# Differential attention among fp32 projections: paired scores, a buffer for four blocks of probabilities, and steps of ScalarE and VectorE in another order

## What is computed

```python
q1 = partial_rope(rmsnorm(qh[..., :64], g_q));  q2 = ...(qh[..., 64:])
k1 = partial_rope(rmsnorm(kh[..., :64], g_k));  k2 = ...(kh[..., 64:])
# for each block of 128 queries, mask: chunk(key) <= chunk(query), chunks of 64
s1 = einsum('bhqd,bhkd->bhqk', q1, k1) / 8
s2 = einsum('bhqd,bhkd->bhqk', q2, k2) / 8
p = softmax(where(mask, s1, NEG_INF)) - lam * softmax(where(mask, s2, NEG_INF))
o_b = rmsnorm(einsum('bhqk,bhkd->bhqd', p, v), g_sub) * (1 - lambda_init)
```

## Time and profile before

| | |
|---|---|
| median of 3 runs | 2455.0 us (2454.37 to 2455.52) |
| profiled execution | 2456.67 us |
| its span, first to last instruction | 2454.8 us |
| TensorE busy | 2385.6 us, 97% |
| VectorE, ScalarE, GpSimd busy | 1309.3 (53%), 870.2 (35%), 239.3 (10%) us |
| mean granted TensorE clock | 0.991 |

### The profile page before, as it was taken

One profiled execution on the slowest core, in us unless ns is written; L12 is line 12 of the kernel. 1 busy time (PEld: TensorE's weight loads), 2 busy tenths in 40 slices (PEclk: granted clock), 3 DMA queues, 4 the chain that ended last, 5 costly groups with the idle time before them and its releaser, 6 DMA issues.

```text
span 2454.8 us, 33629 instructions
## 1 busy us (share of the span) xinstructions
PE 2385.6 (97%) x11140; PEld 1906.9 (78%) x11148; DVE 1309.3 (53%) x1859; ACT 870.2 (35%) x1349; POOL 239.3 (10%) x225
## 2 busy tenths in 40 slices
PE   6999999999999999999999999999999999999997
PEld 4777667888888787776878888887888787888886
DVE  4443665654343559885546455465544545544554
ACT  2454344543232442214333222234444333322222
POOL 3001110112000110001112000021000302000003
PEclk8999999999999999999999999999999999999999
DMA  3111112333333433330213333333121222333332
GB/s 117 52 47 48 52 52 70 98 116 94 94 95 94 121 101 95 111 111 27 85 43 94 96 101 94 94 87 86 53 59 52 65 64 60 103 93 95 99 92 83
DMA packets 394557, 202.36 MB, mean 82 GB/s; under 512 B 13626, under 2 KB 392683, under 8 KB 394474
## 3 DMA queue, kind: packets, MB, share of 16 engines
q1 hardware_dynamic: 393136, 198.56, 27.6%
q0 software_dynamic: 1008, 2.62, 0.3%
q10 hardware_dynamic: 330, 0.08, 0.0%
HBM read 199.11 MB, written 2.10 MB: 82 GB/s over the span
## 4 chain that ended last, share of the span: by engine, by line
PE 88%; DVE 4%; issue 3%; ACT 2%; DVEq 1%; POOLq 0%; DMA 0%; ACTq 0%; SPq 0%; POOL 0%
PE bank L1614 23%; PE bank L1616 22%; PE bank L1615 22%; PE bank L1598 2%; PE bank L1972 2%; PE bank L1964 2%; PE bank L1992 2%; DVE m_w_lo L996 1%; PE bank L2180 1%; PE bank L2071 1%; PE bank L2047 1%; PE bank L2152 1%; PE bank L1733 1%; PE bank L1709 1%; PE bank L1745 1%
## 5 line engine op out<-in xcount | busy, mean ns | idle before, releaser
L517 ACT ACTIVATE m_w_hi<-m_raw 128x1024 fp32r<-128x1024 f32 x341 | 361.3, 1060 | 963.2 <-PE bank L1616 924.2
L1614 PE MATMUL bank<-m_h_hi,m_w_hi 128*128 128x512 f32 x1504 | 619.1, 412 | 9.8 <-DVE m_h_lo L1035 5.8
L1616 PE MATMUL bank<-m_h_hi,m_w_lo 128*128 128x512 f32 x1504 | 588.4, 391 | 0.0
L1615 PE MATMUL bank<-m_h_lo,m_w_hi 128*128 128x512 f32 x1504 | 587.4, 391 | 0.0
L996 DVE TENSOR_TENSOR m_w_lo<-m_raw,m_w_hi 128x1024 fp32r<-128x1024 f32 x341 | 472.7, 1386 | 75.8 <-ACT m_w_hi L517 72.5
L1614 PEld LDWEIGHTS bank<-m_h_hi,m_w_hi 128*128 128x128 f32 x1504 | 283.8, 189 | 83.9 <-issue 25.2
L1616 PEld LDWEIGHTS bank<-m_h_hi,m_w_lo 128*128 128x128 f32 x1504 | 283.0, 188 | 61.1
L1615 PEld LDWEIGHTS bank<-m_h_lo,m_w_hi 128*128 128x128 f32 x1504 | 284.0, 189 | 57.6 <-issue 5.8
L1614 PE MATMUL bank<-m_f_hi,m_w_hi 128*128 128x512 f32 x688 | 269.8, 392 | 2.9 <-DVE m_w_lo L996 2.7
L1616 PE MATMUL bank<-m_f_hi,m_w_lo 128*128 128x512 f32 x688 | 267.8, 389 | 0.0
L1615 PE MATMUL bank<-m_f_lo,m_w_hi 128*128 128x512 f32 x688 | 267.8, 389 | 0.0
(11 more groups left out here) (342 smaller groups left out, 3142.0 us busy)
## 6 DMA issues: line engine op xcount, KB each, us to landing
m_raw<-in_ff_w SPq DMA_DIRECT2D x256, 256.0 KB, 3.0
m_raw<-in_w_in SPq DMA_DIRECT2D x48, 256.0 KB, 3.1
m_raw<-in_conv_pw_w SPq DMA_DIRECT2D x48, 256.0 KB, 4.0
m_raw<-in_w_ffn_gate SPq DMA_DIRECT2D x44, 256.0 KB, 3.1
m_raw<-in_w_ffn_up SPq DMA_DIRECT2D x44, 256.0 KB, 3.2
m_raw<-in_w_ffn_down SPq DMA_DIRECT2D x40, 256.0 KB, 3.0
m_raw<-in_w_gate SPq DMA_DIRECT2D x32, 256.0 KB, 2.9
m_mem_w<-in_mem_wk SPq DMA_DIRECT2D x32, 256.0 KB, 3.1
```

Of the source, the lines that this page charges most:

```text
L517: act.activation(WH[:, v % 2], RAW[:, v % 2], ACT.Copy).then_inc(s.w_hi, 1)
L1614: pe.matmul(o, WH[:, r, k, :], hi, start=start, stop=False)
L1615: pe.matmul(o, WH[:, r, k, :], lo, start=False, stop=False)
L1616: last = pe.matmul(o, WL[:, r, k, :], hi, start=False, stop=stop)
```

## The change

- **TensorE, scores:** `sc(b)` issues both score matmuls, then both masks.
- **TensorE, order:** both `bd` at hook 0.5. `sc(2)` goes from 9 to 8.5, `vt` from 7 to 9.5, `sc(3)` from 11 to 10.5, `tr(0)` from 9 to 11.5, `av(0)` and `tr(1)` to 12.5, `av(1)` from 12 to 13.5, `tr(2)` from 12.5 to 14. `av(2)`, `tr(3)` go from 14 to -0.5 of the next group, `av(3)` from 15 to 1 of it, `turned_o` from 4.5 to 7.
- **Buffer:** `PC` holds the combined probabilities of all four blocks, 1280 columns; `cm` writes there and `tr` reads there.
- **ScalarE:** `squares` and the root of the head before are taken out of `roots` and put behind it, in the first and second list; `pt(3)` goes into the next group; `ex`, `turned_v` and `pt` are in a later and other order.
- **VectorE:** `step` has a second list, `between`, issued between a unit's evacuation and the next split; `mx(3)`, `cm(2)` are in it for the third unit. `on` and `ol` go to the second unit's list, around `mx(0)`, `mx(1)`; `cm(1)` to the third's.

```diff
--- before.py
+++ after.py
@@ -225,6 +225,8 @@
         P1 = at("da_p1", 164, [P, 2, T])
         P2 = at("da_p2", 168, [P, 2, T])
         SQD = at("da_sq", 172, [P, 2, T])
+        BLOCKS = [P * t * (t + 1) // 2 for t in range(QB + 1)]
+        PC = at("da_pc", 72, [P, BLOCKS[QB]])
 
         def staging(tag, kb):
             return [at(f"{tag}_{n}", kb + 2 * i, [P, T]) for i, n in
@@ -635,20 +637,12 @@
 
             def da_pieces(n, prev):
                 def roots():
-
-                    if prev is not None:
-                        squares(prev)
-                        act.drain()
                     for t in range(2):
                         act.wait_ge(s.da_ms, n * 2 + (t + 1))
                         act.activation(RSD[t][:], SBK[t][:], ACT.Ln, bias=EPSC)
-                    if prev is not None:
-                        root_log()
                     act.drain()
                     for t in range(2):
                         act.activation(RSD[t][:], RSD[t][:], ACT.Exp, scale=-0.5).then_inc(s.da_rs, 1)
-                    if prev is not None:
-                        root_exp()
 
                 def ex(b):
                     def f():
@@ -660,17 +654,18 @@
                                            accum_out=ST[:, 8 * b + 2 + c:8 * b + 3 + c]).then_inc(s.da_exp, 1)
                     return f
 
...
-                return [[roots],
-                        da_late(prev)[1:] + [turned_v(V, s.da_vt, s.da_v, n), ex(0), ex(1)],
-                        [pt(0), ex(2), pt(1), ex(3)],
-                        [pt(2), pt(3)]]
+                late = da_late(prev)
+                return [late[0:1] + [roots] + late[1:2],
+                        late[2:3] + [ex(0)] + late[3:],
+                        [ex(1), turned_v(V, s.da_vt, s.da_v, n), ex(2), da_pt(n, 0)],
+                        [ex(3), da_pt(n, 1), da_pt(n, 2)]]
+
+            def da_pt(n, b):
+                def f():
+                    w = (b + 1) * P
+                    act.wait_ge(s.da_tr, n * 4 + (b + 1))
+                    act.activation(PT[:, b % 2, 0:w], TR[:, 0:w], ACT.Copy).then_inc(s.da_pt, 1)
+                return f
 
@@ -686,9 +681,11 @@
 
             def da_late(n):
 
-                def on():
+                def power():
                     squares(n)
                     act.drain()
+
+                def root():
                     root_log()
                     act.drain()
                     root_exp()
@@ -696,7 +693,7 @@
                 def oh():
                     act.wait_ge(s.da_g, n + 1)
                     act.activation(pick(OBH, n), DT2[:], ACT.Copy).then_inc(s.da_oh, 1)
-                return [] if n is None else [on, oh]
+                return [] if n is None else [da_pt(n, QB - 1), power, root, oh]
 
             def then(pieces, late):
                 return [late + pieces[0]] + pieces[1:] if late else pieces
@@ -714,7 +711,7 @@
             with U.loop(act, PAIRS - 2, 4) as i:
                 group([None] * 4, da_pieces(i + 1, i))
             group([None] * 4, da_pieces(PAIRS - 1, PAIRS - 2))
-            group([None] * 4, [da_late(PAIRS - 1), [], [], []])
+            group([None] * 4, [da_late(PAIRS - 1)[0:2], da_late(PAIRS - 1)[2:], [], []])
             act.wait_ge(s.gates_in, 1)
 
 
@@ -996,13 +993,15 @@
                 dve.tensor_tensor(WL[:, v % 2], RAW[:, v % 2], WH[:, v % 2].bitcast(F32), ALU.subtract)\
                     .then_inc(s.w_lo, 1)
 
-            def step(evac, before=()):
+            def step(evac, before=(), between=()):
                 for piece in before:
                     piece()
                 n = U.take()
                 if evac is not None:
                     dve.wait_ge(s.unit_done, U.count(n + 1))
                     evac(GB[n % 2], bank_free[n % 2])
+                for piece in between:
+                    piece()
                 if n + 2 < TOTAL:
                     split(n + 2)
 
@@ -1036,9 +1035,9 @@
                                              in1=pick(hi, m).bitcast(F32), op0=ALU.mult, op1=ALU.subtract)\
                         .then_inc(s.xg_lo, 1)
 
-            def group(evacs, pieces):
+            def group(evacs, pieces, between=((),) * 4):
                 for j, e in enumerate(evacs):
-                    step(e, pieces[j] if pieces else ())
+                    step(e, pieces[j] if pieces else (), between[j])
 
 
             for k in range(KD):
@@ -1176,25 +1175,25 @@
                 def cm(b):
                     def f():
                         w = (b + 1) * P
-                        a, c = P1[:, b % 2, 0:w], P2[:, b % 2, 0:w]
+                        a, c, out = P1[:, b % 2, 0:w], P2[:, b % 2, 0:w], PC[:, BLOCKS[b]:BLOCKS[b + 1]]
                         r = ST[:, 8 * b + 6:8 * b + 8]
                         dve.wait_ge(s.da_exp, n * 8 + (2 * b + 2))
                         dve.reciprocal(r, ST[:, 8 * b + 2:8 * b + 4])
                         dve.drain()
                         dve.tensor_scalar(c, c, r[:, 1:2], LAM, ALU.mult, ALU.mult)
                         dve.drain()
-                        dve.scalar_tensor_tensor(out=a, in0=a, scalar=r[:, 0:1], in1=c,
+                        dve.scalar_tensor_tensor(out=out, in0=a, scalar=r[:, 0:1], in1=c,
                                                  op0=ALU.mult, op1=ALU.subtract).then_inc(s.da_p, 1)
                     return f
 
                 late = da_late(prev)
-                return [[gained(0), gained(1)] + late[0:1] + [rope(0), rope(1)],
-                        late[1:] + [mx(0), mx(1), cm(0), cm(1)],
-                        [mx(2), cm(2), mx(3)],
-                        [cm(3)]]
+                return [[gained(0), gained(1), rope(0), rope(1)],
+                        late[0:1] + [mx(0), mx(1)] + late[1:] + [cm(0)],
+                        [cm(1), mx(2)],
+                        [cm(3)]], ((), (), [mx(3), cm(2)], ())
 
             def then(pieces, late):
-                return [late + pieces[0]] + pieces[1:]
+                return [late + pieces[0][0]] + pieces[0][1:], pieces[1]
 
             def gate(c):
                 return scaled(pick(GATES, c))
@@ -1238,11 +1237,11 @@
             with U.loop(dve, PAIRS - 2, 4) as i:
                 group(sb_evacs(i + 2, (s.sb_vt, i + 2)), sb_pieces(i + 1, i))
             group(da_evacs(0, (s.sb_vt, PAIRS)), sb_pieces(PAIRS - 1, PAIRS - 2, False))
-            group(da_evacs(1, (s.da_vt, 1)), then(da_pieces(0, None), sb_late(PAIRS - 1)))
+            group(da_evacs(1, (s.da_vt, 1)), *then(da_pieces(0, None), sb_late(PAIRS - 1)))
             with U.loop(dve, PAIRS - 2, 4) as i:
-                group(da_evacs(i + 2, (s.da_vt, i + 2)), da_pieces(i + 1, i))
-            group([gate(8 + j) for j in range(4)], da_pieces(PAIRS - 1, PAIRS - 2))
-            group([gate(12 + j) for j in range(4)], [da_late(PAIRS - 1), [], [], []])
+                group(da_evacs(i + 2, (s.da_vt, i + 2)), *da_pieces(i + 1, i))
+            group([gate(8 + j) for j in range(4)], *da_pieces(PAIRS - 1, PAIRS - 2))
+            group([gate(12 + j) for j in range(4)], [[], da_late(PAIRS - 1), [], []])
             dve.drain().then_inc(s.gates_in, 1)
 
             with U.loop(dve, 4, 2) as i:
@@ -1755,8 +1754,32 @@
                         13.5: [c(1, 2)], 14.5: [c(1, 3)]}
                 return merged_hooks(mine, sb_late(prev)) if prev is not None else mine
 
+            def da_tr(n, b):
+                def f():
+                    pe.wait_ge(s.da_p, n * 4 + (b + 1))
+                    if b == 0:
+                        pe.wait_ge(s.da_v, n + 1)
+                    else:
+                        pe.wait_ge(s.da_pt, n * 4 + b)
+                    for j in range(b + 1):
+                        last = turn(TR[:, j * P:(j + 1) * P], PC[:, BLOCKS[b] + j * P:BLOCKS[b] + (j + 1) * P])
+                    last.then_inc(s.da_tr, 1)
+                return f
+
+            def da_av(n, b):
+                def f():
+                    pe.wait_ge(s.da_pt, n * 4 + (b + 1))
+                    if b == 0 and (not isinstance(n, int) or n > 0):
+                        pe.wait_ge(s.da_on, n)
+                    for j in range(b + 1):
+                        last = pe.matmul(OB[:, b * P:(b + 1) * P], PT[:, b % 2, j * P:(j + 1) * P], V[:, j, :],
+                                         start=(j == 0), stop=(j == b))
+                    last.then_inc(s.da_av, 1)
+                return f
+
             def da_late(n):
-                return {4.5: [turned_o(ON, s.da_on, n + 1, s.da_ot)]}
+                return {-0.5: [da_av(n, 2), da_tr(n, 3)], 1: [da_av(n, 3)],
+                        7: [turned_o(ON, s.da_on, n + 1, s.da_ot)]}
 
             def da_hooks(n, prev):
                 def vt():
@@ -1788,39 +1811,17 @@
                         if b >= 2:
                             pe.wait_ge(s.da_exp, n * 8 + (2 * b - 2))
                         for c in range(2):
-                            bank = SBK[(2 * b + c) % 4]
```

(12 more changed lines are left out.)

## The result

| | before | after |
|---|---|---|
| median of 5 runs | 2455.0 us | 2440.3 us (2439.74 to 2442.62) |
| ratio, 95% interval | | 0.9943 (0.9931 to 0.9955) |
| profiled execution | 2456.67 us | 2439.74 us |
| its span | 2454.8 us | 2437.6 us |
| stretch S (below) | 185.3 us | 170.3 us |

The forecast was 2443.4 us, with 2438.5 to 2450.5 as the range, 11.6 us less than before; 14.7 us less were measured. One of the five executions of before took 2687.7 us and is not among the runs that the ratio compares.

The account below looks back on a forecast made before the run. TensorE, busy 97% of the span, was taken as the bound. Paired scores (8.6 us) plus fewer waits (3.0) save 11.6 us: profiled 2456.7 becomes 2445.1, median 1.7 lower, 2443.4; range 2438.5 to 2450.5.

Parts of the forecast that it names:

- The pairing, 8.6 us: In each sc, both scores before both masks save a load, mask switching and one pass: 2.15 us a group, 8.6 in all.
- three passes: In each sc, the two scores' four fp32 passes take the time of three; chance 0.50, 2441 to 2446 us.
- the one from neighbours in the queue to neighbours in time: In sc, passes issued A1, A2, B1, B2 (A, B the row halves): only neighbours A2 and B1 overlap, saving one pass.
- the rival of two passes: In each sc, the scores take two passes in place of four: 15.9 us saved with the waits, 2439.1 us; chance 0.12.
- The waits, 4.8 gone and 1.8 new: TensorE waits for probabilities, m_ob_lo and a split go, 4.8 us; new av(1) waits 0.2, 0.8, 0.8; 3.0 saved.
- `rot(0)`'s 4.0 us and the half clock behind it: In the group without a predecessor, the 4.0 us wait and 3.1 us at clock 0.52 behind it stay unchanged.
- Two table loads at no cost: On ScalarE, the last head's separate squares and root add two 1.28 us table loads a group; no cost, 3 us cover.
- `turned_o` in time with 0.4 of slack: In each group, on is done at 18.0 us and turned_o due at 18.4: slack 0.4, the thinnest.
- the fourth unit's split in time: On VectorE, the split behind ol is done by 26.3 us, needed at 27.8: 1.5 us of cover.
- That is what the buffer of four blocks buys: At tr(3), cm(3) is done at 34.6 us, due about 36.9, so the 2.9 us wait for probabilities goes.
- The sum as two terms that add: Over the whole kernel, 8.6 us from paired scores plus 3.0 from waits give 11.6 us saved.
- The slower rival: VectorE 5.5 us later at the fourth unit's split, behind on and turned_o, loses 5.5 us a group: 2460 us; chance 0.05.

Follow-up runs that it names:

- experiment 1: Changed kernel with each score matmul again followed by its own mask: 2449.44 us, ratio 0.9974.
- experiment 3: Changed kernel with each score matmul cut into two of half the columns, both of rows 0 to 63 issued first: 2439.53 us, ratio 0.9935.
- experiment 5: Changed kernel with ScalarE's pt(0) before ex(2) and pt(1) before ex(3), and tr(0) at hook 11: 2436.28 us, ratio 0.9922.
- experiment 6: Changed kernel with head 0's roots ahead of oh on ScalarE and gained ahead of ol on VectorE: 2434.62 us, ratio 0.9918.
- experiment 9: Changed kernel with ScalarE's copies and head 0's roots moved ahead, mx(3) and cm(2) issued behind the third unit's split: 2440.26 us, ratio 0.9940.
- experiment 8: Changed kernel with ScalarE's copies and head 0's roots moved ahead, combined probabilities back in the two-block buffer, no PC: 2430.45 us, ratio 0.9901.
- A B A B: Changed kernel with each score matmul cut into two of half the columns, issued alternating between the two row halves: 2442.57 us, ratio 0.9946.

## Why the prediction was right, and where not

- **The pairing, 8.6 us: right mechanism, wrong size.** Hidden loads, cheaper mask switches and overlapped passes are there; the passes are two, not three. From the first load of `sc(3)` to the mask it is 1.07 us, where three passes had 1.47 and two 1.05. The term measures 13.2 by the prices of the `sc` (experiment 1); the upper bound was 12.9. The step that failed is the one from neighbours in the queue to neighbours in time: B1 need not wait for A2, as experiment 3 shows with whole instructions. The 4.6 us that this adds are more than the difference of 11.6 and 15.1; the waits give 0.6 less than forecast.
- **The number in the range: partly luck.** The case taken as most likely, three passes at 0.50 with 2441 to 2446, did not happen. What happened is the rival of two passes, given 0.12 and 2439.1. The measured 2440.3 lies in the range because its lower end had been put just under that rival.
- **The waits, 4.8 gone and 1.8 new: 4.8 gone and 2.4 new.** Gone are exactly the three kinds that were named. Of the new ones, `av(1)` was forecast at 0.2, 0.8, 0.8 and 0; measured 0.24, 0.60, 0.60 and none. For `av(0)` no wait was forecast; it waits 0.60 and 0.35 in the second and third group. The cause named, ScalarE's copies behind late exponentials, is borne out by experiment 5. A recorded wait is not the whole price: taking these 2.4 us away shortens S by 3.9 at an equal clock.
- **`rot(0)`'s 4.0 us and the half clock behind it stay:** right, and that its cause is the place of `oh` and `ol` in line, ahead of head 0's roots and products, is shown by experiment 6. How long the half clock lasts differs between traces with the same wait.
- **Two table loads at no cost, `turned_o` in time with 0.4 of slack, the fourth unit's split in time:** right, no wait for any of them stands in the view.
- **"That is what the buffer of four blocks buys": not borne out.** The buffer alone does not remove the waits for the probabilities: with it in place but nothing between evacuation and split they are 7.4 us (experiment 9). And the copies-first order does without the third and fourth block (experiment 8). In the changed kernel's own order the buffer lets `ex(2)` run ahead of `tr(0)`; what it is worth there is open.
- **The sum as two terms that add: right only for the pair.** Each was worked out with the other in place, and so came close; alone they are worth 2.7 to 4.2 us of S and nothing. A reader who took the pairing's term for its price in the old order would be wrong by all of it.
- **The slower rival**, a slip behind `on` and `turned_o`, did not occur.

## To carry to other kernels

An engine that is 97% busy can still be paced by a chain that is just as long; before a saving on it is booked, ask for each wait behind it how much earlier its source can come, and change the order together with the cost. Work whose inputs are there should not stand in line behind a step that waits for another engine: the short copies, `mx(3)` and the roots were worth 4, 10 and 5 us of S by their place alone. Matmuls with a contraction of 64 rows should be issued side by side, with full-height matmuls such as masks gathered behind them.

## What was not expected of the hardware

- Two fp32 matmuls on different 64-row halves, each of two records, run fully beside each other: 1.07 us for both, loads included, 1.06 for one. The order of issue between the halves made no difference (A A B B and A B A B both 1.07).
- In the kernel before with paired scores, two waits of 1.1 and 1.5 us with some 0.9 us of work between them were followed by 4.2 us at a mean granted clock of 0.59. In the kernel with the roots first, `rot(0)`'s wait of 0.8 us was followed by a clock of 1.00.
- The same wait of 4.0 us, in kernels that hardly differ up to there, was followed by a short or a long stretch at the half clock: the mean granted clock from 241.0 to 252.6 us is 0.85 in before (with and without paired scores), changed and A A B B, and 0.71 in interleaved, A B A B and copies first. Through this alone single traces of two kernels differ by 0.9 to 1.5 us.
- Ahead of the changed stretch, in code that is the same in all of them, the traces differ by up to 3.5 us: its first step starts at 231.84 us before and at 228.37 us in the kernel before with paired scores. Two medians 3 us apart (A A B B and A B A B) go with stretches S 0.8 us apart, and two 9.1 us apart (changed and interleaved) with stretches 12.4 us apart.
